# Sums of squares of 16 heads: one full-precision product by ones, or two one-pass products of rounded parts

## The reference, cut to what matters

```python
def rmsnorm(x, w):
    xf = x.astype(jnp.float32)
    y = xf * lax.rsqrt(jnp.mean(jnp.square(xf), axis=-1, keepdims=True) + EPS)
    return (y * w.astype(jnp.float32)).astype(x.dtype)

def l2norm(x):
    xf = x.astype(jnp.float32)
    return xf * lax.rsqrt(jnp.sum(jnp.square(xf), axis=-1, keepdims=True) + EPS)

o_hg = rmsnorm(o_hg, hg_norm) * jax.nn.silu(heads(hog, HG_DV).astype(jnp.float32))
q = l2norm(heads(cq, GDN_DK)) * GDN_DK ** -0.5
k = l2norm(heads(ck, GDN_DK))
o_gdn = rmsnorm(o_gdn, gdn_norm) * jax.nn.silu(heads(gz, GDN_DV).astype(jnp.float32))
```

## Time and profile before

| | |
|---|---|
| median of 3 runs | 950.32 us (949.94 to 951.69) |
| profiled execution | 952.0 us |
| its span in the trace | 950.2 us |
| granted TensorE clock, mean | 0.998 |
| transfers, mean over the span | 110 GB/s |

### The profile page before, as it was taken

One profiled execution on the slowest core, in us unless ns is written; L12 is line 12 of the kernel. 1 busy time (PEld: TensorE's weight loads), 2 busy tenths in 40 slices (PEclk: granted clock), 3 DMA queues, 4 the chain that ended last, 5 costly groups with the idle time before them and its releaser, 6 DMA issues.

```text
span 950.2 us, 22427 instructions
## 1 busy us (share of the span) xinstructions
PE 925.2 (97%) x9441; PEld 893.8 (94%) x9441; DVE 664.1 (70%) x1248; ACT 434.8 (46%) x800; POOL 102.6 (11%) x131
## 2 busy tenths in 40 slices
PE   5999999999999999999999999999999999999997
PEld 5999888989999999999999999999999999999996
DVE  3778879866577677477766888789435899994453
ACT  6687445424223544553223257355323666662213
POOL 0110011112020110100100000122001222220000
PEclk9999999999999999999999999999999999999999
DMA  9834233344433432315643332232233343323222
GB/s 346 270 84 136 59 97 112 114 127 118 116 101 102 123 85 68 100 56 168 204 128 106 89 90 85 71 90 73 85 96 104 101 121 90 90 78 101 67 68 95
DMA packets 146174, 104.88 MB, mean 110 GB/s; under 512 B 5169, under 2 KB 138999, under 8 KB 144923
## 3 DMA queue, kind: packets, MB, share of 16 engines
q1 hardware_dynamic: 139099, 79.23, 28.4%
q0 software_dynamic: 6352, 22.00, 7.5%
q10 hardware_dynamic: 624, 2.23, 0.6%
HBM read 100.12 MB, written 3.31 MB: 109 GB/s over the span
## 4 chain that ended last, share of the span: by engine, by line
PE 54%; ACT 1%; DVE 1%; issue 1%; POOL 0%; ACTq 0%; POOLq 0%; DVEq 0%
PE G L2155 35%; PE G L2245 19%; PE R L2166 0%; POOL w_sum L1165 0%; PE R L2289 0%; PE R L2163 0%; DVE w_lo L1593 0%; ACT o_hi L1227 0%; ACT w_hi L1220 0%; ACT L1548 0%; ACT ytok L1483 0%; DVE val L2117 0%; DVE val L2015 0%; DVE ya L2063 0%; DVE val L2068 0%
## 5 line engine op out<-in xcount | busy, mean ns | idle before, releaser
L2155 PE MATMUL G<-h_hi,w_hi 128*128 128x272 f32 (+1 forms) x912 | 272.9, 299 | 1.6 <-ACT inp L1519 0.8
L2155 PE MATMUL G<-h_lo,w_hi 128*128 128x272 f32 (+1 forms) x912 | 263.1, 288 | 0.4 <-issue 0.4
L2155 PE MATMUL G<-h_hi,w_lo 128*128 128x272 f32 (+1 forms) x912 | 262.7, 288 | 0.1
L1593 DVE TENSOR_TENSOR w_lo<-raw,w_hi 128x1024 fp32r<-128x1024 f32 (+2 forms) x113 | 119.2, 1055 | 105.4 <-ACT w_hi L1220 104.6
L2155 PEld LDWEIGHTS G<-h_hi,w_hi 128*128 128x128 f32 x912 | 171.7, 188 | 5.0 <-issue 1.0
L2155 PEld LDWEIGHTS G<-h_lo,w_hi 128*128 128x128 f32 x912 | 172.0, 189 | 0.6 <-issue 0.6
L2155 PEld LDWEIGHTS G<-h_hi,w_lo 128*128 128x128 f32 x912 | 171.7, 188 | 0.0
L1220 ACT ACTIVATE w_hi<-raw 128x1024 fp32r<-128x1024 f32 (+2 forms) x113 | 103.6, 916 | 100.2 <-PE G L2155 100.1
L1165 POOL TENSOR_TENSOR w_sum<-raw 128x512 f32<-128x512 f32 x34 | 47.1, 1388 | 321.5 <-DMA raw<-in_w_up 181.7
L2245 PE MATMUL G<-x_hi,sum_hi 128*128 128x272 f32 x272 | 78.8, 290 | 1.5 <-ACT partial L1323 1.5
L2245 PE MATMUL G<-x_hi,sum_lo 128*128 128x272 f32 x272 | 78.7, 289 | 0.0
(11 more groups left out here) (328 smaller groups left out, 2050.2 us busy)
## 6 DMA issues: line engine op xcount, KB each, us to landing
raw<-in_w_in SPq DMA_DIRECT2D x48, 512.0 KB, 4.1
raw<-in_w_up SPq DMA_DIRECT2D x44, 512.0 KB, 4.0
w_ada<-in_w_ada_t POOLq DMA_DIRECT2D x49, 256.0 KB, 3.0
wada<-in_w_ada_s SPq DMA_DIRECT2D x8, 1024.0 KB, 13.9
raw<-in_w_down SPq DMA_DIRECT2D x16, 320.0 KB, 3.1
raw<-in_w_out SPq DMA_DIRECT2D x8, 512.0 KB, 4.1
raw<-in_w_down SPq DMA_DIRECT2D x8, 512.0 KB, 4.1
w_ada_t<-in_w_ada_t POOLq DMA_DIRECT2D x15, 256.0 KB, 3.1
```

The costliest lines, as they stand in the source:

```text
L1593: dve.tensor_tensor(lo, raw[:, i % RAW, 0:job.nk, 0:job.m], hi.bitcast(F32), ALU.subtract).then_inc(w_lo_done, 1)
L2155: ins = pe.matmul(out, w, x, start=(job.first and k == 0 and p == 0), stop=(job.last and k == job.nk - 1 and p == 2))
```

## The change

ACT squares each head twice, once into `sq` in float32 and once into `sq_hi`, where the same square is rounded to float32r. DVE subtracts the one from the other into `sq_lo`, where it squared before. PE adds the two parts up in one PSUM group, with ones in float32r, in two one-pass products for each group of columns. `sq_hi` lies in the memory of `val`, `sq_lo` in that of `sq`. A new semaphore, `squared`, goes from ACT to DVE. GpSimd fills the ones at the start of the program, and their transfer is gone.

```diff
@@ tiles
-        ones = sb("ones", [P, P])
+        ones = sb("ones", [P, P], F32R)
+        sq_hi = nc.alloc_sbuf_tensor_at("sq_hi", [P, 2, TOK], F32R, offset=val_at)
+        sq_lo = nc.alloc_sbuf_tensor_at("sq_lo", [P, 2, TOK], F32R, offset=sq_at)
@@ SyncE, GpSimd
-            sp.dma_start(ones[:, :], t["all_ones"]).then_inc(const_in, 16)
+            pool.memset(ones[:, :].bitcast(F32), 1.0).then_inc(ones_set, 1)
@@ ScalarE
+            def square(n, x):
+
+                j = sq_no[n] % 2
+                act.activation(sq[:, j, :], x, ACT.Square)
+                act.activation(sq_hi[:, j, :], x, ACT.Square).then_inc(squared, 1)
...
                 elif name == "g_sq":
                     if seen["conv"] in (conv_no[a] + 1, 12):
                         conv_silu()
+                    pair, k = a
+                    act.wait_ge(conv_ready, conv_no[pair, k] + 1)
+                    square(n, inp[:, pair, k, :])
+                elif name == "o_sq":
+                    hd = a[0]
+                    wait_bank(act, last_bank[spot("h_o" if hd < NH else "g_o", hd % NH // 2, 3)])
+                    square(n, o[:, hd, :])
@@ VectorE
+            def square_lo(n):
+
+                j = sq_no[n] % 2
+                dve.wait_ge(squared, sq_no[n] + 1)
+                dve.tensor_tensor(sq_lo[:, j, :], sq[:, j, :], sq_hi[:, j, :].bitcast(F32), ALU.subtract).then_inc(sq_ready, 1)
...
                 elif name == "g_sq":
-                    pair, k = a
-                    dve.wait_ge(conv_ready, conv_no[pair, k] + 1)
-                    x = inp[:, pair, k, :]
-                    dve.tensor_tensor(sq[:, sq_no[n] % 2, :], x, x, ALU.mult).then_inc(sq_ready, 1)
+                    square_lo(n)
@@ TensorE
-            def sums_of(n, k, x):
-                fill(n, k, [mm(lambda b: R[:, b, 0:SEQ], ones[:, :], x[:, 0:SEQ])])
-                fill(n, k + 1, [mm(lambda b: R[:, b, 0:DEC], ones[:, :], x[:, SEQ:TOK])])
+            def sums_of(n, k, hi, lo):
+                for j, cols_ in enumerate(GROUPS):
+                    fill(n, k + j, [mm(lambda b: R[:, b, 0:cols_.stop - cols_.start], ones[:, :], hi[:, cols_], True, False),
+                                    mm(lambda b: R[:, b, 0:cols_.stop - cols_.start], ones[:, :], lo[:, cols_], False, True)])
```

More of the change, by code:

```diff
@@ L631, in build @@
         sel = nc.alloc_sbuf_tensor_at("sel", [NH, NH, P], F32, offset=rn_at)
+        sq_at = (nc.sbuf_base + 31) // 32 * 32
         sq = sb("sq", [P, 2, TOK])
         acc = sb("acc", [P, TOK])
+        val_at = (nc.sbuf_base + 31) // 32 * 32
         val = sb("val", [P, 2, TOK])
+        sq_hi = nc.alloc_sbuf_tensor_at("sq_hi", [P, 2, TOK], F32R, offset=val_at)
+        sq_lo = nc.alloc_sbuf_tensor_at("sq_lo", [P, 2, TOK], F32R, offset=sq_at)
         base = (nc.sbuf_base + 31) // 32 * 32
@@ L799, in build @@
         const_in = sem("const_in")
+        ones_set = sem("ones_set")
+        squared = sem("squared")
         vec_in = sem("vec_in")
@@ L1368, in _ @@
                     act.wait_ge(pad_zero, 3)
-                    act.wait_ge(const_in, 48)
+                    act.wait_ge(ones_set, 1)
+                    act.wait_ge(const_in, 32)
                     act.activation(sel_r[0:NH, :, :], sel[:, :, :], ACT.Copy)
@@ L1392, in _ @@
                     link(act.activation(rows[:, 1, :], rows[:, 1, :], ACT.Exp))
-                    act.activation(rows[:, 1, :], rows[:, 1, :], ACT.Ln, bias=ones[0:NH, 0:1]).then_inc(sp_log, 1)
+                    act.activation(rows[:, 1, :], rows[:, 1, :], ACT.Ln, bias=ones[0:NH, 0:1].bitcast(F32)).then_inc(sp_log, 1)
                 elif name == "g_a":
@@ L1833, in _ @@
                         ins = dve.tensor_tensor_scan(rows[:, 3, toks(c)], rows[:, 0, toks(c)],
-                                                     ones[0:NH, 0:length(c)], 1.0, ALU.mult, ALU.mult)
+                                                     ones[0:NH, 0:length(c)].bitcast(F32), 1.0, ALU.mult, ALU.mult)
                     ins.then_inc(pg_ready, 1)
@@ L1999, in _ @@
                 elif name == "o_sq":
-                    hd = a[0]
-                    wait_bank(dve, last_bank[spot("h_o" if hd < NH else "g_o", hd % NH // 2, 3)])
-                    dve.tensor_tensor(sq[:, sq_no[n] % 2, :], o[:, hd, :], o[:, hd, :], ALU.mult).then_inc(sq_ready, 1)
+                    square_lo(n)
                 elif name == "o_scale":
@@ L2261, in _ @@
                     if a == duos[0]:
-                        pe.wait_ge(const_in, 48)
+                        pe.wait_ge(ones_set, 1)
+                        pe.wait_ge(const_in, 32)
                     rest = range(KD - 2 if a == duos[0] else SUMS_AT, KD)
@@ L2288, in added @@
                             pe.wait_ge(acc_ready if last else acc_part, 1)
-                            return pe.matmul(R[:, b, 0:cols_.stop - cols_.start], ones[:, :], x[:, cols_],
+                            return pe.matmul(R[:, b, 0:cols_.stop - cols_.start], ones[:, :].bitcast(F32), x[:, cols_],
                                              start=not last, stop=last, skip_group_check=True)
@@ L2295, in _ @@
                     pe.wait_ge(acc_ready, 2 + turn)
-                    fill(n, 0, [mm(lambda b, c=c: R[0:length(c), b, 2 * c:2 * c + 2], x[:, toks(c)], ones[:, 0:2], x is acc, x is not acc)
+                    fill(n, 0, [mm(lambda b, c=c: R[0:length(c), b, 2 * c:2 * c + 2], x[:, toks(c)], ones[:, 0:2].bitcast(F32), x is acc, x is not acc)
                                 for c in chunks for x in (acc, sq[:, 0, :])])
@@ L2305, in _ @@
                     pe.wait_ge(sq_ready, head_norms[n] + 1)
-                    sums_of(n, 0, sq[:, head_norms[n] % 2, :])
+                    j = head_norms[n] % 2
+                    sums_of(n, 0, sq_hi[:, j, :], sq_lo[:, j, :])
                 elif name == "g_rows":
@@ L2490, in constants @@
     low = np.tile(low, (P // QUAD, 1, 1)).astype(np.float32)
-    return {"level_masks": np.stack(levels, 1).astype(np.float32), "level_masks_t": low, "unit_c": unit, "level_masks_c": small, "all_ones": np.ones((P, P), np.float32),
+    return {"level_masks": np.stack(levels, 1).astype(np.float32), "level_masks_t": low, "unit_c": unit, "level_masks_c": small,
             "head_select": select}
```

## The result

The changed kernel took 954.67 us, the median of 7 runs (952.95 to 955.20), against 950.85 us for 7 runs of the kernel before (949.94 to 951.69). The ratio is 1.0029, with a 95% interval from 1.0017 to 1.0041: **slower by 0.3%**, or 3.8 us by the medians. Eight kernels were run afterwards in two groups of four, beside which the kernel before had medians of 951.52 (30 runs) and 951.43 us (28 runs).

A forecast was written before the change was run, and what follows sets the result against it. The prediction took PE to bound the kernel, busy for 925.2 of 950.2 us. Its terms, +1.5 + 1.9 - 2.1 = +1.3 us, took the median from 950.32 to 951.6 us, with an 8-in-10 range of 947.0 to 955.5.

The forecast's parts named there:

- slower: Whole kernel: the case of a time slower by over 0.2%, above 952.2 us; chance 0.41.
- three rivals: Block as dear as `g_bcast`'s (0.12), ACT's lateness reaching the first `g_gram` (0.20), new products costing what float32 did (0.03).
- What PE saves: Sums of each of 16 heads: the block takes 0.61 us instead of 0.99, 0.38 us less a head.
- the rival of a block as dear as `g_bcast`'s: Sums of each head: the one-pass block saves only 0.20 us a head, giving 953.6 us; chance 0.12.
- What ACT gets: Two squares of 544 elements a head on ACT, 0.64 us each; a pair holds up the next instruction by 1.22 us.
- Heads (0,2) to (0,1): 58 to 95 us: PE waits in `g_bcast` for the Ln behind the squares; 1.5 us late after four heads.
- that rival: ACT's lateness reaches the first `g_gram`, where PE waits: 952.5 us, up to 955; chance 0.20.
- Heads (1,2) to (1,1): 143 to 171 us: late `u_tok` costs 2.06 us at (1,3), 0.51 at (1,1); together +1.9 us.
- The eight output heads: 272 to 403 us: savings of 2.93 us less 0.85 lost between two levels, together -2.1 us.
- The level: PE's next level at 360.35 us, among the output heads: chain 1.6 us late, 0.8 to spare, so +0.85 us.
- The sum: Whole kernel: +1.5 + 1.9 - 2.1 = +1.3 us, median 951.6 us.
- The waits don't form: Squares run while ACT is idle and nothing stands behind them: all 16 heads save 0.38, 944.2 us; chance 0.15.

The follow-up runs named there:

- PE kept busy: The changed kernel with 18 unread products of 272 columns on PE ahead of the wait for `u_tok` near 153.4 us; 952.56 us, ratio 1.0017.
- the products alone: Against the kernel before: DVE squares once into float32r, PE multiplies that part twice, no squares on ACT, low part left out; 948.93 us, ratio 0.9970.
- squares_first: The changed kernel with the two ACT squares of head (1,3) ahead of the other head's silu instead of behind it; 951.81 us, ratio 1.0002.
- two_plain: The changed kernel with heads (0,3) and (0,0) as before: DVE squares, float32 product, nothing on ACT; 952.79 us, ratio 1.0014.
- the changed kernel's second trace: The changed kernel run again unaltered, beside the kernel with 18 unread products on PE, on the same chip; 954.43 us, ratio 1.0034.

## Why the prediction was right and wrong

The time lies inside the range (947.0 to 955.5) and above the forecast's own (949.5 to 953.5), and it fell into "slower", to which I gave 0.41. By the spans the forecast was +1.3 us and the traces say +2.7. That it fell into "slower" is no merit of mine: the 0.41 stood for three rivals and the upper end of my own range, and none of the three rivals happened. What took the time above the forecast, the clock and the savings that were not kept, had no place in it, and the range held because it reached over rivals that would have cost as much for other reasons.

- **What PE saves.** Right. 0.24 us for 512 columns, 0.61 for the block, 0.38 a head, so the rival of a block as dear as `g_bcast`'s falls: the steps of the lag at output heads are 0.38 to 0.41. My estimate from the four passes of the Trainium skill ("FP8 and Floating Point Precision", TensorE Precision Notes) was 0.43; no head shows that much.
- **What ACT gets.** Right. The square of `inp` lasts 0.64 us, and the other starts 0.55 behind it. For the wait at (1,3), timelines of ACT and DVE:

```profile
152.65 0.63 ACT L1242 ACTIVATE inp<-cy 128x512 f32<-128x512 f32 x1 [3.05 <-DVE cy L1855]
...
153.30 0.64 ACT L1262 ACTIVATE sq<-inp 128x544 f32<-128x544 f32 x1
153.85 0.64 ACT L1263 ACTIVATE sq_hi<-inp 128x544 fp32r<-128x544 f32 x1
...
154.52 0.72 DVE L1662 TENSOR_TENSOR sq_lo<-sq,sq_hi 128x544 fp32r<-128x544 f32 x1 [1.91 <-ACT sq_hi L1263]
```

- **Heads (0,2) to (0,1): +1.5.** Measured +1.27 at `PT`. The wait in `g_bcast` is there, released by ACT's `rn`, but a little shorter: PE was to be ready at 70.1 and released at 72.07, 1.97 us, and it waits 1.64; the projection behind it starts 1.14 us late (72.21 against 71.07), not 1.28. The Ln started at 71.15, not 71.38. No PE wait at a `g_gram` shows up, so that rival falls too.
- **Heads (1,2) to (1,1): +1.9.** Each wait came out as worked out: 0.42 + 2.06 + 0.38 = 2.86 us for `u_tok` of (1,3), measured 2.83; 0.51 + 0.38 = 0.89 us at (1,1), measured 0.89. (The second match is partly luck, since the sum knew nothing of the low clock ahead of it; with PE kept busy the same wait is 0.73.) But the lag, read at DVE's `w_lo` on either side of the stage, grew from 1.1 to 4.2 us. The step that failed is "`u_tok` ... goes from 152.69 to 154.75 ...: 2.06 us late". It prices a wait of PE at its length, on the silent assumption that PE goes on behind it at the full clock, and the term lacks 1.6 us. With PE kept busy the stage costs +1.5, a little under the forecast.
- **The eight output heads: -2.93 + 0.85.** The level was right: 0.75 us of wait, 0.83 of lag. The savings were mis-sized: the lag falls by 0.40, 0.38, 0.41, 0.39, 0.13, 0.40, and by nothing for the last two, 2.1 us in all. The fifth doesn't lose its 0.27 us to ACT's squares: with the products alone it gives no more (lag -2.03 at 369.27, -2.17 at 380.28). Its Ln on ACT stands behind `gate_mid` and a table load, and starts 2.14 us after the sums do in either kernel, whatever the sums cost. PE's group with `masks`, which follows shortly behind the sums, takes 0.2 us longer than before:

```profile
374.54 0.86 ACT L1248 ACTIVATE rn<-R,eps 128x512 f32<-128x512 f32 x2
374.62 1.25 PE L2166 MATMUL R<-masks,inp 128*128 128x128 f32 x10
```

```profile
377.34 1.45 PE L2187 MATMUL R<-masks,inp 128*128 128x128 f32 x10
377.66 0.87 ACT L1254 ACTIVATE rn<-R,eps 128x512 f32<-128x512 f32 x2
```

The first two rows are of before, the others of the changed kernel. 0.2 us of the saving end in this group, which fits a fill that waits until Ln has read its bank; no listed wait says so, and it isn't shown. The last two do save 0.63 us at their place (2.08 us from 400.55 to the next projection at 402.63, now 1.45 from 403.14 to 404.59), but they give it back at 418.15, in the wait for `w_lo`, which was 0.60 and is now 1.18. The step behind it is in the first paragraph: "there is no idle time later that could take it up", read from a busy share of 534 in 544 us. A share that high still held two waits of 0.6 us.
- **The sum.** 1.27 + 3.1 - 1.28, less 0.5 us that the lag falls between the stages (0.2 near 118 us, 0.3 near 214), is 2.6 us, and the trace has 2.65. Near both places PE has waits without a releaser ("issue"), 2.5 us in all before and 1.8 in the changed kernel; they differ from kernel to kernel. The two misses, 1.6 for the clock and 0.8 for the savings, are partly made up by stages that came out 0.2 and 0.4 us cheaper and by those 0.5 us.
- **The waits don't form** (0.15) was not so; `squares_first` shows what one wait less gives: 0.3 us above before by the medians, where the changed kernel is 3.0 and 3.8 us above.

## What to carry to other kernels

An engine that is idle for half of the time is no cover by itself. What decides is what stands in its queue at the moment of use, and work moved onto it is to be priced at the instruction behind it. On TensorE a wait is not priced at its length alone: behind a long one look at the granted clock, and if it falls, make the wait shorter by reordering, or fill it. A saving counts only if the next wait is not there already: before summing equal savings, walk from each one to the next place where the engine waits.

## What the runs showed of the hardware

The clock falls behind waits much shorter than I had thought worth a line. It fell behind all four waits of PE near 2.8 us: 2.83 us (0.56 and 0.58 in the next two stretches of 2 us), 2.83 in `two_plain` (0.50 for 6 us), 2.82 in the changed kernel's second trace (0.50 from 158 to 160 us), and 2.69 (0.52, 0.62). Of shorter waits it fell behind four: 2.15 us in `squares_first` ahead of 23.29 us (0.60 and 0.55 from 24 to 28 us), 1.65 us with PE kept busy (below), and these two, without a releaser as the first:

```profile
23.14 2.26 PE L2184 MATMUL R<-wada,c_cols 128*32 128x128 f32 x55 [2.10 <-issue]
```

```profile
217.19 0.45 PE L2200 MATMUL R<-Xc,Uc 32*32 32x32 f32 x25 [1.55 <-issue]
```

The first is of the changed kernel's second trace, which reads 0.70 and 0.73 from 23 to 29 us; the second is of the kernel with two heads as before (0.68 and 0.75 from 217 to 223 us), and its lag grows by 1.7 us there. But the trace of before has 2.09 us idle at the first place and stays at 1.00, and the wait for `rn` in `g_bcast`, of 1.64, 1.65 and 1.64 us in the changed kernel's two traces and in `squares_first`, leaves it at 1.00. So the same idle time brings the clock down in one run and not in another; a part of the spread of before (949.52 to 955.27 in 28 runs) may come from that, which was not traced. The longest wait of PE, 7.2 us ahead of its first product, says little: the column reads 1.00 there, yet PE does 6 or 7 products in each us from 8 to 11 us and about 10 from then on (trace of before), so it isn't shown that the column holds for the start. The Trainium skill ("TensorE: Matmul & The Clock Gate", Part 1: The HAM clock gate) has the same two levels and says that the gate follows how busy PE has been of late; the stretches of 0.50 and 1.00 agree with the levels, and no run shows what it counts.

A fallen clock need not cost anything. With PE kept busy at `u_tok`, the trace has the clock at 0.63 from 74 to 78 us, behind the 1.65 us wait for `rn`, and its lag grows by 1.26 us from 36 to 97 us, as much as that of the changed kernel (1.26), which kept 1.00. PE then waits for `PT` for 0.27 us in place of 0.88: the slower products only used up a wait that was to come.
